# The prompt's attention scores of two heads, from zero-padded queries to two row tiles of 64 partitions

## The chip, the cores and the metric

The kernel runs on one core of one Trainium2 chip. A core has five engines that matter here: TensorE (PE in the profile, with its weight loads listed apart as PEld), VectorE (DVE), ScalarE (ACT), GpSimd (POOL) and SyncE (SP), which issues the DMAs. The metric is the device time of one execution in microseconds (us). Before the change it is 2594.43 us, the median of 3 runs from 2592.45 to 2596.81 us.

## The reference

The reference is one step of a two-layer decoder trunk, for a prompt of 1024 tokens and for 8 sequences of 8 sample tokens. Layer 0 is a Mamba-2 mixer, layer 1 is dilated sliding-window attention. The change touches only the attention of the prompt. Cut to that:

```python
DILATION_GROUPS = ((128, 1), (512, 4), (2048, 16))     # window, dilation
ATT_HEAD_DIM, ATT_HEADS, ATT_KV_HEADS = 64, 16, 4      # 4 query heads share a key head
def dilated_attend(q, kv_groups, rows_groups):
    for gi in range(N_DGROUPS):
        ...                                            # kg, vg: the keys and values of the window
        s = jnp.einsum('bqkrd,bqjkd->bqkrj', qg, kg)   # scores, contracted over 64
        s = jnp.where(valid[None, :, None, None, :], s, -jnp.inf)
        lse = jax.nn.logsumexp(s, axis=-1)
        pr = jnp.exp(s - lse[..., None])
        o = jnp.einsum('bqkrj,bqjkd->bqkrd', pr, vg)
        ...
    # the three groups are then merged by a softmax over their lse
```

## The kernel before

The attention of the prompt is stage 4. Its queries are taken in 24 units: 3 dilation groups of 8 units, each unit 128 query rows that have the same residue of the dilation. A unit sees either the keys of its own 128 rows alone (OWN, 13 units) or those of the 128 rows before it too (FULL, 11 units). `units4` runs them in this order: unit 0 OWN, 1 to 7 FULL, then 8 to 16 OWN and FULL in turn, then 17 to 23 OWN.

A unit has 8 steps, one for each pair of heads (a pair holds two query heads, `x` = 0 and 1, whose key heads lie in the lower and the upper 64 partitions of the same key tile). So stage 4 has 192 steps, 88 of FULL units and 104 of OWN units. For step A, each engine's program holds:

- PE (`section4_tensor`): the scores of step A (line 1837, one product per head, 256 columns in a FULL unit, 128 in an OWN unit; 4 instructions), then `turn_scores` for step A-2 (line 1801, transposes of the exponentials), then `values` for step A-3 (line 1818), and after steps 1, 3 and 5 of a unit one part of `turn` (lines 1788 and 1792), which transposes keys and queries of the next unit.
- DVE (`section4_vector`): mask and row maximum of step A for each head (line 1712), the negated maximum (line 1716), then `evacuate`, which copies the turned exponentials of step A-2 out of PSUM bank 6 (line 1696).
- ACT (`section4_scalar`): the exponentials of step A (line 1618); now and then `take`, which copies turned keys (line 1582) and queries (line 1586) from bank 7 into `kT` and `qT`, and `hand_out` (line 1595).

The scores go to banks 0 to 3, one bank for each head of two steps. The order on each engine is that of the code; the engines wait on semaphores. `turn_scores` of step A-1 waits until `evacuate` of step A-2 has freed bank 6; that in turn follows the mask of step A on DVE.

Before the change `qT` has, for each pair and each head, a full 128-partition block of which the other head's 64 partitions are zero. The product over 128 partitions then gives one head's scores. GpSimd writes these zeros once (line 1546), before anything else of stage 4, and ScalarE fills the 64 partitions of each head in a copy of its own (line 1586).

Of the kernel before, what the change touches and what calls it, by code (L numbers as in the profile page):

```python
# [25 lines left out]
P = 128  # L26
# [13 lines left out]
DI, HD, NH, NG, DS = 2048, 64, 32, 4, 128  # L40
# [12 lines left out]
AH, KVH, REP = 16, 4, 4  # L53
# [77 lines left out]
def trunk_kernel(nc, a, o, s):  # L131

    outer = ExitStack()
    with outer:
        def sem(name):
            return outer.enter_context(nc.semaphore(name))

        def sb_in(ctx):
            def sb(name, shape, dt=F32):
                return ctx.enter_context(nc.sbuf_tensor(name, shape, dt))  # L140
            return sb

        keep = sb_in(outer)
        bank = outer.enter_context(nc.psum_tensor("bank", [P, 8, 512], F32))
# [15 lines left out]
        h = keep("h", [P, NT, D])  # L160
# [78 lines left out]
        sb = sb_in(s1)  # L239
# [111 lines left out]
        def alone(eng):  # L351

            eng.sem_inc(q["waits_passed"], 1)
# [103 lines left out]
        def turn_of(i, times, const):  # L458

            return const if i is None else i * times + const  # L460
# [405 lines left out]
        def stage2_vector(dve, chain):  # L866
# [97 lines left out]
        sb = sb_in(s4)  # L964
        HP = AH // 2
# [2 lines left out]
        kn = sb("kn", [P, 2, KVH * HD])  # L968
        vv = sb("vv", [P, 2, 2, KVH * HD])
        kT = sb("kT", [P, 2, KVH // 2, 2, P])  # L970
        qT = sb("qT", [P, 2, HP, 2, P])
        win = sb("win", [P, 2 * P])
        pair = sb("pair", [P, P])
        sc = sb("sc", [P, 4, 512])
# [20 lines left out]
        f4 = {n: sem("att_" + n) for n in """m_landed s_full masked p_ready t_full pt_ready pv_done u_taken tr_full  # L995
            tr_ready kp_ready zeroed qz_landed os_stored qzs_ready
            ktr_full ktr_ready ss_full ss_masked se_ready rd_ready st_full spt_ready so_full so_ready schain""".split()}
# [84 lines left out]
        def third(pool, t):  # L1082

            pool.wait_ge(f5["w_ready"], t + 1)
            v = u6[t % 2][:, 2, :].rearrange("p (h d) -> p h d", h=AH)
            pool.tensor_tensor(v, v, bc(wts[:, t % 2, 4, 2, :], P, AH, HD), ALU.mult).then_inc(f5["third"], 1)
# [296 lines left out]
        def units4(eng, body):  # L1383

            body(None, 0, OWN, None, 0)
            body(None, 1, FULL, OWN, 1)
            with eng.Fori(0, 3) as i:
                body(i, 2, FULL, FULL, 1)
                body(i, 3, FULL, FULL, 2)
            body(None, 8, OWN, FULL, 0)  # L1390
            body(None, 9, FULL, OWN, 5)
            with eng.Fori(0, 3) as i:
                body(i, 10, OWN, FULL, 0)
                body(i, 11, FULL, OWN, 6)
            body(None, 16, OWN, FULL, 0)
            body(None, 17, OWN, OWN, 0)
            with eng.Fori(0, 2) as i:
                body(i, 18, OWN, OWN, 0)
                body(i, 19, OWN, OWN, 0)
            body(None, 22, OWN, OWN, 0)  # L1400
            body(None, 23, OWN, OWN, 0)

        def sequences(eng, body):

            with eng.Fori(0, NSEQ // 2 - 2) as i:
                for d in range(2):
                    body(i, d)
            for d in range(NSEQ - 4, NSEQ):
                body(None, d)
# [15 lines left out]
        def section4_sync(sp):  # L1425
# [13 lines left out]

            def load_queries(kv):  # L1440

                sp.wait_ge(f4["zeroed"], 3)
                for x in range(kv * REP, (kv + 1) * REP):
                    for g in range(NGR):
                        at = (x // (2 * REP) * 2 * REP + x % REP * 2 + kv % 2) * HD
                        src = s["q"][SEQ:TOK, g, at:at + HD].rearrange("(s t) d -> t s d", t=DSEQ)
                        sp.dma_start(qz[x * DSEQ:(x + 1) * DSEQ, :, g, kv // 2, (kv % 2) * HD:(kv % 2 + 1) * HD], src).then_inc(f4["qz_landed"], 16)
# [18 lines left out]
            def body(i, un, kind, before, nth):  # L1466
# [17 lines left out]
                if un in EARLY:  # L1484
                    load_queries(EARLY.index(un))
# [55 lines left out]

        def section4_gpsimd(pool):
            pool.wait_ge(j3["full"], UNITS3)
            for x in range(2):
                other = slice(64 * (1 - x), 64 * (1 - x) + 64)
                pool.memset(qT[other, :, :, x, :], 0.0).then_inc(f4["zeroed"], 1)
                pool.wait_ge(f4["zeroed"], x + 1)
            pool.memset(qz, 0.0).then_inc(f4["zeroed"], 1)

            def body(i, un, kind, before, nth):  # L1550
                if un < UN - 1:
                    nx = un + 1
                    pool.wait_ge(f4["tr_ready"], turn_of(i, 6, 3 * un + 1))
                    pool.wait_ge(f4["s_full"], turn_of(i, 32, 16 * un))
                    alone(pool)
                    pool.tensor_copy(kT[:, nx % 2, :, 0, :], kT[:, un % 2, :, 1, :]).then_inc(f4["kp_ready"], 1)

            units4(pool, body)
            pool.wait_ge(f4["qz_landed"], 16 * AH * NGR)
            pool.wait_ge(f4["t_full"], HP * UN)  # L1560

            def pick(i, d):

                if d > 1 or i is not None:
                    pool.wait_ge(f4["ktr_full"], turn_of(i, 14, 7 * max(0, d - 1)))
                alone(pool)
                pool.tensor_copy(qzs[:, d % 2, :, :, :], qz[:, bass.ds(turn_of(i, 2, d), 1), :, :, :].rearrange("p s g a d -> p (s g) a d")).then_inc(f4["qzs_ready"], 1)

            sequences(pool, pick)
            third(pool, 0)  # L1570
            third(pool, 1)

        def section4_scalar(act):

            def take(i, un, part):

                sl = un % 2
                act.wait_ge(f4["tr_full"], turn_of(i, 6, 3 * un + part + 1))
                if part == 0:
                    if un:  # L1580
                        act.wait_ge(f4["kp_ready"], turn_of(i, 2, un - 1))
                    act.copy(kT[:, sl, :, 1, :], bank[:, 7, 0:2 * P].rearrange("p (h n) -> p h n", h=2)).then_inc(f4["tr_ready"], 1)
                else:
                    for x in range(2):
                        hs_ = slice(64 * x, 64 * x + 64)
                        last = act.copy(qT[hs_, sl, 4 * (part - 1):4 * part, x, :], bank[hs_, 7, :].rearrange("p (h n) -> p h n", h=4))  # L1586
                    last.then_inc(f4["tr_ready"], 1)

            def hand_out(i, un, part):

# [4 lines left out]
                act.copy(ub[:, sl, part * 512:(part + 1) * 512], bank[:, 4 + part, :]).then_inc(f4["u_taken"], 1)  # L1595

            act.wait_ge(j3["rot_ready"], UNITS3)
            act.wait_ge(f4["zeroed"], 2)
            for part in range(3):
                take(None, 0, part)  # L1600

# [176 lines left out]
        def section4_tensor(pe):  # L1778
# [16 lines left out]
            def turn_scores(i, st0, kind):  # L1795
                pe.wait_ge(f4["p_ready"], turn_of(i, 16, st0 + 1))
                if st0 > 0:
                    pe.wait_ge(f4["pt_ready"], turn_of(i, 16, st0))
                for x in range(2):
                    for k in range(kind):  # L1800
                        last = pe.transpose(bank[:, 6, (x * kind + k) * P:(x * kind + k + 1) * P],  # L1801
                                            sc[:, st0 % 4, 256 * x + k * P:256 * x + (k + 1) * P], ident)
                last.then_inc(f4["t_full"], 1)
# [23 lines left out]
            def body(i, un, kind, before, nth):  # L1827
                sl, n = un % 2, kind * P
                pe.wait_ge(f4["tr_ready"], turn_of(i, 6, 3 * (un + 1)))
                if un:  # L1830
                    pe.wait_ge(f4["kp_ready"], turn_of(i, 2, un))
                for j in range(HP):
                    st0 = HP * un + j
                    if st0 > 1:
                        pe.wait_ge(f4["masked"], turn_of(i, 16, st0 - 1))
                    for x in range(2):
                        pe.matmul(bank[:, 2 * (st0 % 2) + x, 0:n], qT[:, sl, j, x, :],  # L1837
                                  kT[:, sl, j // REP, 2 - kind:2, :].rearrange("p a n -> p (a n)"), start=True, stop=True).then_inc(f4["s_full"], 1)
                    if st0 > 1:
                        turn_scores(i, st0 - 2, kind if j > 1 else before)  # L1840
                    if st0 > 2:
                        if j > 2:
                            values(i, un, j - 3, kind, nth)
                        else:
                            values(i, un - 1, j + HP - 3, before, 0)
                    if j in (1, 3, 5) and un < UN - 1:
                        turn(i, un + 1, j // 2)
# [217 lines left out]
        def _(pool):  # L2065
# [10 lines left out]
            with pool.Fori(0, NG) as g:  # L2076
# [36 lines left out]
                root(g * NT + LC, ROWS[LC])  # L2113
            stage2_gpsimd(pool)
            section4_gpsimd(pool)
            stage6_gpsimd(pool)

# [658 lines left out]
```

## Time and profile before

| what | value |
|---|---|
| median of 3 runs | 2594.43 us (2592.45 to 2596.81) |
| profiled execution, its own time | 2597.51 us |
| its span, first to last instruction | 2595.7 us |
| mean granted clock of TensorE | 0.969 of full speed |
| busy shares of the span | PE 94%, PEld 78%, DVE 55%, ACT 42%, POOL 17% |
| stage 4, first scores to the end of its last values | 1824.5 to 2195 us |

The page's busy shares are means over stages that differ; a matmul's end in the trace is modelled, and matmuls overlap one another, so PE counted as busy is not PE at its peak. How long a row of matmuls really holds PE is seen from the chain of work that ended last: there a group's time runs to the start of the next group, not to its own modelled end.

### The profile page before, as it was taken

Reading aid. Unit: us, or ns where it says so; the run is one execution under the profiler, and the core shown is the slowest. Engines: PE = TensorE matmul, PEld = TensorE weight load, DVE = VectorE, ACT = ScalarE, POOL = GpSimd, SP = SyncE. Lnnn points to the kernel's source line nnn. Section 1 sums busy time; section 2 is a strip of 40 time slices with the busy share of each in tenths; the row PEclk is TensorE's granted clock in tenths of the full one; section 3 lists DMA queues with packets and bytes.
Section 4 is the critical chain, followed back from the end, with each engine's and each line's share of the span. In section 5 each row is a group of like instructions: output and inputs, shape, how many; then the busy total and the mean of one; then the engine's idle time right before and its main releaser. Section 6 shows DMA issues by size and latency. Waiting matters only on the chain.

```text
span 2595.7 us, 38609 instructions
## 1 busy us (share of the span) xinstructions
PE 2429.4 (94%) x12776; PEld 2013.0 (78%) x12776; DVE 1427.7 (55%) x3033; ACT 1082.8 (42%) x2453; POOL 435.5 (17%) x327
## 2 busy tenths in 40 slices
PE   4699999999999779999999999999999988989998
PEld 3697797797798468887788888887898887667776
DVE  3267567667567413333463777751566665267632
ACT  3146346346346412332332333331667777353211
POOL 0006106106106100000120333310000000001100
PEclk8799999999999689999999999999999999889999
DMA  3032232232222653420142422321333347855210
GB/s 114 11 110 71 75 112 70 81 107 72 82 89 75 203 152 82 114 101 33 41 148 82 167 79 79 109 83 53 89 90 83 90 101 176 247 157 198 105 56 21
DMA packets 233453, 259.96 MB, mean 100 GB/s; under 512 B 33639, under 2 KB 176127, under 8 KB 233304
## 3 DMA queue, kind: packets, MB, share of 16 engines
q1 hardware_dynamic: 233304, 258.01, 32.8%
q8 instruction: 89, 1.46, 0.2%
q14 instruction: 60, 0.49, 0.1%
HBM read 192.46 MB, written 69.29 MB: 101 GB/s over the span
## 4 chain that ended last, share of the span: by engine, by line
PE 82%; DVE 7%; DMA 4%; issue 3%; ACT 2%; SPq 2%; POOL 0%; DVEq 0%; ACTq 0%; POOLq 0%
PE bank L781 7%; PE bank L780 7%; PE bank L782 7%; PE bank L1837 3%; PE bank L1818 3%; PE bank L2538 3%; PE bank L2539 3%; PE bank L2540 3%; PE bank L607 2%; PE bank L608 2%; PE bank L609 2%; PE bank L2592 2%; PE bank L1801 2%; PE bank L2705 2%; PE bank L2594 2%
## 5 line engine op out<-in xcount | busy, mean ns | idle before, releaser
L780 PE MATMUL bank<-wh,uH 128*128 128x512 f32 x792 | 308.5, 389 | 0.0
L782 PE MATMUL bank<-wh,uL 128*128 128x512 f32 x792 | 308.1, 389 | 0.0
L781 PE MATMUL bank<-wl,uH 128*128 128x512 f32 x792 | 308.1, 389 | 0.0
L1618 ACT ACTIVATE sc<-sc,nmx 128x128 f32<-128x128 f32 (+1 forms) x384 | 169.7, 443 | 98.5 <-DVE nmx L1716 97.2
L2538 PE MATMUL bank<-uH,wxh 128*128 128x364 f32 (+1 forms) x504 | 167.1, 331 | 10.1 <-DVE wxl L2351 10.1
L782 PEld LDWEIGHTS bank<-wh,uL 128*128 128x128 f32 x792 | 148.6, 188 | 30.9
L780 PEld LDWEIGHTS bank<-wh,uH 128*128 128x128 f32 x792 | 148.7, 188 | 30.8
L781 PEld LDWEIGHTS bank<-wl,uH 128*128 128x128 f32 x792 | 148.7, 188 | 30.7
L2539 PE MATMUL bank<-uL,wxh 128*128 128x364 f32 (+1 forms) x504 | 166.4, 330 | 0.0
L2540 PE MATMUL bank<-uH,wxl 128*128 128x364 f32 (+1 forms) x504 | 166.2, 330 | 0.0
L1837 PE MATMUL bank<-kT,qT 128*128 128x128 f32 (+1 forms) x768 | 162.1, 334 | 1.4 <-ACT qT L1586 1.4
L2094 POOL TENSOR_TENSOR mix<-mix,cbm 128x1024 f32<-128x1024 f32 (+1 forms) x36 | 95.6, 2657 | 374.0 <-DVE cbm L2405 372.0
L703 POOL TENSOR_TENSOR hs<-hs,mhalf 128x8 f32<-128x8 f32 (+1 forms) x54 | 108.5, 2009 | 236.4 <-DVE hs L936 236.4
L1818 PE MATMUL bank<-vv,pT 128*128 128x64 f32 x1120 | 146.8, 266 | 0.1
L1818 PEld LDWEIGHTS bank<-vv,pT 128*128 128x128 f32 x1120 | 140.1, 192 | 0.6 <-DVE pT L1696 0.3
L1712 DVE CUSTOM_DVE_ANT_0 sc<-bank,win 128x256 f32<-128x256 f32 (+1 forms) x256 | 87.9, 381 | 89.8 <-PE bank L1837 77.5
L607 PE MATMUL bank<-woh,yh 128*128 128x512 f32 x288 | 115.8, 402 | 16.4 <-DVE yl L581 13.9
L2592 PE MATMUL bank<-wzh,uH 128*128 128x512 f32 x288 | 125.1, 434 | 3.5 <-ACT zs L2238 3.5
L1837 PEld LDWEIGHTS bank<-kT,qT 128*128 128x128 f32 x768 | 116.4, 194 | 6.4 <-issue 1.7
L854 ACT ACTIVATE raws<-bank,rstd 128x512 f32<-128x512 f32 (+1 forms) x54 | 37.1, 688 | 197.3 <-PE bank L782 178.9
L608 PE MATMUL bank<-wol,yh 128*128 128x512 f32 x288 | 114.3, 397 | 0.0
L609 PE MATMUL bank<-woh,yl 128*128 128x512 f32 x288 | 113.9, 396 | 0.0
(341 smaller groups left out, 5624.5 us busy)
## 6 DMA issues: line engine op xcount, KB each, us to landing
mix<-scratch_acum SPq DMA_DIRECT2D x32, 512.0 KB, 3.8
yin<-scratch_yT SPq DMA_DIRECT2D x16, 1024.0 KB, 5.9
wr<-in_a_in_w SPq DMA_DIRECT2D x16, 1024.0 KB, 7.5
wx<-in_m_in_w SPq DMA_DIRECT2D x24, 512.0 KB, 3.9
scratch_q<-rot SPq DMA_DIRECT2D x48, 256.0 KB, 2.0
qn<-scratch_q SPq DMA_DIRECT2D x48, 256.0 KB, 3.5
scratch_u<-ub SPq DMA_DIRECT2D x48, 256.0 KB, 2.9
u<-scratch_u SPq DMA_DIRECT2D x24, 512.0 KB, 5.4
```

The costliest lines, as they stand in the source:

```text
L607: pe.matmul(to, high[:, k, :], woh[j][:, k, :], start=(k == 0), stop=False)
L608: pe.matmul(to, high[:, k, :], wol[j][:, k, :], start=False, stop=False)
L780: pe.matmul(bank[:, t % 3, :], high, whigh, start=(k == 0), stop=False)
L781: pe.matmul(bank[:, t % 3, :], high, wlow, start=False, stop=False)
L782: last = pe.matmul(bank[:, t % 3, :], low, whigh, start=False, stop=(k == KT - 1))
L1618: last = act.activation(v, v, ACT.Exp, bias=nmx[:, sl, head(j, x):head(j, x) + 1], accum_out=mxs[:, sl, AH + head(j, x):AH + head(j, x) + 1])
L1818: last = pe.matmul(bank[:, 4 + hd // 8, (hd % 8) * HD:(hd % 8 + 1) * HD], pT4[:, st0 % 2, (x * kind + k) * P:(x * kind + k + 1) * P], vv[: ...
L1837: pe.matmul(bank[:, 2 * (st0 % 2) + x, 0:n], qT[:, sl, j, x, :], kT[:, sl, j // REP, 2 - kind:2, :].rearrange("p a n -> p (a n)"), start=T ...
L2538: pe.matmul(to, wxh[:, f % 2, k, :], uH[:, k, c0:c1], start=(k == 0), stop=False)
L2539: pe.matmul(to, wxh[:, f % 2, k, :], uL1[:, k, c0:c1], start=False, stop=False)
L2540: last = pe.matmul(to, wxl[:, f % 2, k, :], uH[:, k, c0:c1], start=False, stop=(k == KT - 1))
L2592: pe.matmul(bank[:, 4, :], uH[:, k, ts], wzh[:, k, :], start=(k == 0), stop=False)
```

## The change

`qT` holds both heads of a pair in one block: head 0 in partitions 0 to 63, head 1 in 64 to 127, without zeros. The scores of a head are then one product over 64 partitions, `rows` 0 to 63 or 64 to 127 of both operands, so that the two products of a pair use two row tiles of the array. The two zeroing memsets and the waits for them go, and `take` copies a part of the queries in one copy over 128 partitions in place of two over 64. A block `below_win` fills the memory that `qT` gives up, so that all other tiles stay where they were.

```diff
-        qT = sb("qT", [P, 2, HP, 2, P])
+        qT = sb("qT", [P, 2, HP, P])
+        sb("below_win", [P, 2 * HP * P])
...
-                sp.wait_ge(f4["zeroed"], 3)
+                sp.wait_ge(f4["zeroed"], 1)
...
-            for x in range(2):
-                other = slice(64 * (1 - x), 64 * (1 - x) + 64)
-                pool.memset(qT[other, :, :, x, :], 0.0).then_inc(f4["zeroed"], 1)
-                pool.wait_ge(f4["zeroed"], x + 1)
             pool.memset(qz, 0.0).then_inc(f4["zeroed"], 1)
...
-                    for x in range(2):
-                        hs_ = slice(64 * x, 64 * x + 64)
-                        last = act.copy(qT[hs_, sl, 4 * (part - 1):4 * part, x, :], bank[hs_, 7, :].rearrange("p (h n) -> p h n", h=4))
-                    last.then_inc(f4["tr_ready"], 1)
+                    act.copy(qT[:, sl, 4 * (part - 1):4 * part, :], bank[:, 7, :].rearrange("p (h n) -> p h n", h=4)).then_inc(f4["tr_ready"], 1)
...
-            act.wait_ge(f4["zeroed"], 2)
...
                     for x in range(2):
-                        pe.matmul(bank[:, 2 * (st0 % 2) + x, 0:n], qT[:, sl, j, x, :],
-                                  kT[:, sl, j // REP, 2 - kind:2, :].rearrange("p a n -> p (a n)"), start=True, stop=True).then_inc(f4["s_full"], 1)
+                        rows = slice(HD * x, HD * (x + 1))
+                        pe.matmul(bank[:, 2 * (st0 % 2) + x, 0:n], qT[rows, sl, j, :],
+                                  kT[rows, sl, j // REP, 2 - kind:2, :].rearrange("p a n -> p (a n)"), start=True, stop=True).then_inc(f4["s_full"], 1)
```

On ScalarE, from the queries of unit 0 to those of unit 1 (COPY into `qT` are the queries, ACTIVATE the exponentials), before:

```order
L1582 COPY kT<-bank 128x2x128
L1586 COPY qT<-bank 64x4x128 x4
L1618 ACT_TABLE_LOAD
L1618 ACTIVATE sc,mxs<-sc,nmx 128x128 x4
L1582 COPY kT<-bank 128x2x128
L1618 ACTIVATE sc,mxs<-sc,nmx 128x128 x4
L1586 COPY qT<-bank 64x4x128 x2
```

The same place after the change:

```order
L1579 COPY kT<-bank 128x2x128
L1581 COPY qT<-bank 128x512 x2
L1611 ACT_TABLE_LOAD
L1611 ACTIVATE sc,mxs<-sc,nmx 128x128 x4
L1579 COPY kT<-bank 128x2x128
L1611 ACTIVATE sc,mxs<-sc,nmx 128x128 x4
L1581 COPY qT<-bank 128x512
```

Each pair of copies into `qT` has become one; nothing else moved. On TensorE, in unit 1, the scores, the transposes and the values stand in the same order after the change as before. After it:

```order
L1831 MATMUL bank<-kT,qT 128x256 x2
L1794 MATMUL bank<-cst,sc 128x128 x2
L1811 MATMUL bank<-vv,pT 128x64 x2
L1781 MATMUL bank<-cst,kn 128x128 x2
L1831 MATMUL bank<-kT,qT 128x256 x2
L1794 MATMUL bank<-cst,sc 128x128 x4
```

The sizes that the rows give are those of the output; what changed is that each of the two products of a step now has 64 rows of weights, and that everything between two such pairs still has 128.

## Rows read from the trace of the kernel before

**Rows 1.** The page: span, engines' busy time, and granted clock in 40 slices.

```profile
span 2595.7 us, 38609 instructions
PE 2429.4 (94%) x12776; PEld 2013.0 (78%) x12776; DVE 1427.7 (55%) x3033; ACT 1082.8 (42%) x2453; POOL 435.5 (17%) x327
...
PEclk8799999999999689999999999999999999889999
```

**Rows 2.** Busy time in four stretches of stage 4.

```profile
core 0: us, PE busy (x) PEld busy (x) DVE busy (x) ACT busy (x) POOL busy (x), PEclk, DMA share, GB/s
1824.50:1836.16 11.66, 10.78 (x74) 10.26 (x75) 7.21 (x46) 10.01 (x35) 0.40 (x1) 0.82 0.26 64
1836.16:1966.34 130.18, 129.77 (x952) 116.93 (x952) 90.11 (x336) 86.00 (x274) 2.80 (x7) 1.00 0.34 81
1966.34:2107.07 140.73, 131.75 (x1020) 120.25 (x1020) 95.61 (x434) 101.08 (x351) 3.60 (x9) 1.00 0.38 90
2107.07:2195.00 87.93, 76.05 (x634) 70.63 (x633) 60.53 (x339) 71.42 (x273) 2.00 (x5) 1.00 0.56 133
```

**Rows 3.** Waits in stage 4 (1824.5 to 2195 us): total, times, longest.

```profile
PEld bank L1801 <- issue: 36.9, 88, 0.8
PE bank L1801 <- DVE pT L1696: 18.3, 55, 0.6
```

**Rows 4.** The chain in FULL unit 2 (start, us, what).

```profile
1863.55 0.87 PE bank L1837 x4
1864.41 0.44 PE bank L1801 x4
1864.85 0.84 PE bank L1818 x8
1865.69 0.92 PE bank L1837 x4
```

**Rows 5.** The chain in OWN unit 19.

```profile
2142.32 0.45 PE bank L1837 x4
...
2143.71 0.44 DVE pT L1696
2144.14 0.14 issue
2144.28 0.41 PE bank L1801 x2
```

**Rows 6.** The chain in the Mamba stage, around products over 64 partitions.

```profile
669.93 1.09 PE bank L2683 x8
671.01 0.59 PE bank L2667 x4
671.60 0.44 PE bank L2608 x4
```

**Rows 7.** Timeline of weight loads, transposes of 128 and 24 rows in turn.

```profile
2198.28 0.14 PEld L1873 LDWEIGHTS bank<-cst,ck 128*128 128x128 f32 x1 [0.42 <-ACT uT L1640]
2198.54 0.13 PEld L1874 LDWEIGHTS bank<-cst,nk 24*128 24x128 f32 x1
2198.70 0.14 PEld L1873 LDWEIGHTS bank<-cst,ck 128*128 128x128 f32 x1
```

**Rows 8.** Timeline of weight loads of products with 8 columns (line 2630).

```profile
178.24 0.96 PEld L2630 LDWEIGHTS bank<-cst,u 64*128 64x128 f32 x8 [0.23 <-issue]
```

**Rows 9.** Groups by line and shape, stage 4.

```profile
L1586 ACT COPY qT<-bank 64x512 f32<-64x512 f32 x92 | 53.0, 576 | 1.2
L1595 ACT COPY ub<-bank 128x512 f32<-128x512 f32 x47 | 26.9, 573 | 0.6
```

**Rows 10.** The chain at the start of stage 4.

```profile
1814.56 3.86 DMA kn<-scratch_kv
...
1820.84 0.58 ACT qT L1586
```

**Rows 11.** Timeline, GpSimd's zeros in `qT`.

```profile
1812.74 3.82 POOL L1546 MEMSET qT<- 64x2048 f32 x2 [92.25 <-PE bank L782]
```

## The prediction

> **What bounds the kernel now.** I read the page first, then the chain of waits around line 1837, then stage 4 cut into stretches. The page says that PE is busy 94% of the span and that the clock stands at its upper level through stage 4 [rows 1]. That is a mean; what a shorter or longer score product is worth depends on the stretch [rows 2]. In units 1 to 7 (FULL, 56 steps) PE is busy 129.77 of 130.18 us: every 0.1 us that PE gains or loses in a step arrives at the end. In units 8 to 16 (32 FULL and 40 OWN steps) it idles 9.0 of 140.7 us, in units 17 to 23 (56 OWN steps) 11.9 of 87.9 us. These waits are of one kind: the transposes of line 1801 wait 55 times for DVE's copy of line 1696, and their weight loads stand idle 36.9 us in 88 places [rows 3]. The chain shows the pattern as pairs of steps [rows 5]: scores of step A (0.45 us), then DVE's mask and copy until 2144.14, then `turn_scores` of A-1 at 2144.28, values, a part of `turn`, and the scores of A+2. The scores of A+1 lie inside the 1.5 us between 2142.77 and 2144.28, in which PE has only those scores, two transposes and four values to do; they are off the path.
>
> **What a step costs now.** In a FULL unit four score instructions hold PE for 0.87 to 0.92 us, so 0.22 each, in an OWN unit 0.45, so 0.11 each; eight values hold it 0.84, four transposes 0.44 [rows 4, 5].
>
> **What the change adds: two changes of the array's shape in each step.** The scores now have 64 rows of weights, the transposes and values around them 128. The Mamba stage already does this, in a place where four transposes take the 0.44 us that they take in stage 4. There eight products over 64 partitions with 128 columns hold PE 1.09 us, where eight score instructions of the same columns take 2 x 0.45 = 0.90: going in costs 0.19. The four transposes behind them take 0.59 where the next four take 0.44 [rows 6]: coming out costs 0.15 [rows 6]. That is 0.34 for a round trip. The other bound is a pair of transposes of 128 and 24 rows, whose loads are 0.42 us apart [rows 7]; at 0.11 each they should be 0.22 apart, so two changes cost 0.20 there. I take 0.30 for a round trip, near the first, which has the very form of the new product. What I see in both is that a load does not start under the last product of the other shape, as it does otherwise; the price is that uncovered time.
>
> **What it may take away: two tiles at work at once.** No row here shows two row tiles side by side, so this is bounded. A step's four instructions stand in the order head 0 first pass, head 0 second pass, head 1 first pass, head 1 second pass. If products start in order and one tile does one at a time, only head 0's second and head 1's first pass can overlap: a step of four becomes one of three, a gain of one instruction, 0.22 (FULL) or 0.11 (OWN). The bounds are 0 and two instructions, 0.44 and 0.22. In OWN steps a load is as long as a product: eight products of only 8 columns still need loads over 0.96 us, about 0.11 each [rows 8]. If the loads of the two tiles follow one another, the OWN step gains nothing. I take one instruction for FULL and none for OWN.
>
> The Trainium skill says in TensorE: Matmul & The Clock Gate, section "The mechanism", that products start and end in program order and that a weight load may be drawn ahead where row groups differ; that is the overlap of one instruction. In its section "Measured speedup vs the span model" packed tiles take as long as one product plus about 4 ns for each tile; by that rule the gain would be two instructions, and no run here shows it yet.
>
> **ScalarE, GpSimd, SyncE.** The 92 copies of 64x512 that the stretch holds (0.576 us each, 53.0 us) become 46 of 128x512; ACT's own copy of that size takes 0.573 [rows 9]. ACT loses about 26 us of work, but no wait of PE in stage 4 ends on it [rows 3], so this is worth nothing after the start. At the start two such pairs lie on the chain, of copies of 0.58 [rows 10]: 2 x 0.6 = 1.2 us gained. The memsets ended at 1816.56, before the first keys landed at 1818.42 [rows 10, 11], and the code issues the sample part's queries, the other waiter for them, only from unit 8 on; both are worth nothing.
>
> **The sum, against the profiled execution (2597.5 us).**
> - Units 1 to 7: 56 x (0.30 - 0.22) = +4.5.
> - Units 8 to 16: I count half of the steps as saturated: 16 FULL x 0.08 = +1.3, 20 OWN x 0.30 = +6.0. The others go in pairs, where only the change into the scores of A lies on the path, while the idle 0.4 to 0.8 us in front of line 1801 takes up the rest: 10 OWN pairs x 0.19 = +1.9, 8 FULL pairs x (0.19 - 0.22) = -0.2. Together +9.0.
> - Units 17 to 23: 28 pairs x 0.19 = +5.3.
> - Unit 0: 4 x 0.30 + 2 x 0.19 = +1.6. The start: -1.2.
>
> Sum: +19.2, so 2616.7. That execution is 3.1 us above the median of the runs; on the median it is 2613.6, so 2614 us. With the round trip between 0.20 and 0.34 this case runs from about 2600 to 2618: 96 saturated steps and 48 pairs move with it.
>
> **Rivals.**
> 1. The tiles do not overlap at all, and the change does not do what it says. Without the 0.22 in 72 saturated FULL steps and 8 pairs the sum is +36.8: 2631 us. For it: between a load and its product and the next load all rows here go one after another. Against it: the two tiles share no partition and no PSUM bank.
> 2. The loads overlap too, so that OWN steps also gain one instruction: 24 saturated steps and 40 pairs x 0.11 = 7.0 less, +12.2: 2607 us; with the round trip at 0.20 this is about no change.
> 3. Faster: each tile runs its two instructions beside the other's. Beyond my case 80 x 0.22 + 64 x 0.22 = 31.7 less, -12.5: 2582 us. It decides as soon as head 1's first pass starts with head 0's first, and then the 0.44 of a FULL step beats the round trip. Against it speaks the order of the four; nothing in the trace shows it.
> 4. Going from one tile to the other waits too. No overlap, and 0.15 more in 96 steps and 48 pairs: 36.8 + 21.6 = +58: 2653 us. The Trainium skill speaks against it: in TensorEngine Tiling (Array Packing), section "Key Properties", only a change of the mode drains, not one of the tile.
>
> **Chances.** My case 0.38, no overlap 0.24, loads overlap 0.18 (0.08 of it within 0.2% with the cheap round trip), full overlap 0.13, a wait between the tiles 0.07. 0.2% is 5.2 us, what a measurement here can tell from no change. A remainder of 0.01 goes to faster: 0.14 faster, 0.08 same, 0.78 slower. The range from 2596 to 2635 takes in my case, no overlap and overlapping loads with both ends of the round trip, some 0.8 together; it leaves out rivals 3 and 4.
>
> **What the profile after would show.** Right: the weight loads of the scores and of the transposes behind them each start some 0.2 us after the product before them, in every step; a FULL step without `turn` takes about 2.2 us where it took 2.14 (1863.55 to 1865.69) [rows 4]; head 1's first product starts together with head 0's second; in units 17 to 23 the idle time in front of the transposes shrinks and the pair grows by 0.2; the copies of queries take 0.57 each, 48 of them. Wrong: loads that go on under the products of the other shape, or all four score products of a FULL step done within 0.45 us (rival 3), or each started only when the one before has ended (rivals 1 and 4).

## The result: 0.2% slower, by the clock

| | before | changed |
|---|---|---|
| median of 20 runs | 2594.84 us (2589.40 to 2600.51) | 2601.97 us (2592.20 to 2639.80) |
| ratio, 95% interval | | 1.0022 [1.0012, 1.0031] |
| profiled execution, its span | 2597.51, 2595.7 us | 2602.58, 2600.8 us |
| mean granted clock | 0.969 | 0.964 |
| stage 4, first scores to last values | 1824.53 to 2195.79 (371.25) | 1820.10 to 2203.20 (383.10) |

Here and below the ratio counts only executions within 1.5% of the fastest of their kernel, and the medians count all; where the two differ, the executions left out are those with the lowest mean clock.

The change costs 5.1 us of span: stage 4 begins 4.4 us earlier, lasts 11.85 us longer, and what follows it takes 2.3 us less. The page after, to be laid beside [rows 1]; in its second row PEld has fallen from 2013.0 to 1975.0 us:

```profile
span 2600.8 us, 38559 instructions
PE 2429.0 (93%) x12776; PEld 1975.0 (76%) x12776; DVE 1431.4 (55%) x3033; ACT 1051.2 (40%) x2405; POOL 431.8 (17%) x325
...
PEclk8799999999999789999999999999899989989999
```

The same four stretches as in [rows 2], changed kernel (the columns are those of rows 2):

```profile
1820.10:1837.87 17.77, 15.42 (x75) 12.07 (x75) 7.52 (x46) 9.50 (x34) 0.40 (x1) 0.50 0.32 79
1837.87:1964.90 127.03, 126.00 (x952) 99.40 (x951) 90.08 (x337) 75.76 (x260) 2.80 (x7) 0.97 0.36 83
1964.90:2114.88 149.98, 139.69 (x1019) 112.10 (x1018) 95.31 (x433) 89.87 (x333) 3.60 (x9) 0.91 0.36 85
2114.88:2203.20 88.32, 77.45 (x639) 63.06 (x639) 60.97 (x339) 62.69 (x261) 2.68 (x6) 1.00 0.57 134
```

Units 1 to 7 took 130.18 us and take 127.03; units 17 to 23 took 88.7 to their last values and take 88.3. The loss sits in unit 0 (11.63 to 17.76 us) and in units 8 to 16 (140.7 to 150.0), just where the clock column has fallen most: from 0.82 to 0.50 and from 1.00 to 0.91. In units 1 to 7 it has fallen to 0.97, in units 17 to 23 it is 1.00 in both kernels. Cut finer, before has one stretch at 1.2 GHz around stage 4, from 1815.1 for 13.7 us; after has three, from 1811.9 for 34.1, from 1982.6 for 10.2 and from 2081.6 for 17.1 us.

**At the upper clock the step is shorter.** The chain in FULL unit 3, to be laid beside [rows 4]:

```profile
1881.06 0.84 PE bank L1811 x8
1881.90 0.63 PE bank L1831 x4
1882.54 0.02 issue
1882.56 0.63 PE bank L1794 x4
1883.19 0.84 PE bank L1811 x8
1884.03 0.44 PE bank L1785 x4
1884.47 0.63 PE bank L1831 x4
1885.10 0.59 PE bank L1794 x4
```

Scores 0.87 to 0.92 have become 0.63, transposes 0.44 have become 0.58 to 0.63. The step without `turn` lasts 2.06 (1875.45 to 1877.51) where it lasted 2.14, the one with `turn` 2.57 (1881.90 to 1884.47) where it lasted 2.68, and each of the units 2 to 7 is 0.83 to 0.94 us shorter. The weight loads and products of one step, from the timeline (start, length of the group, what):

```profile
1859.44 0.30 PEld L1831 LDWEIGHTS bank<-kT,qT 64*128 64x128 f32 x4
1859.45 0.70 PE L1831 MATMUL bank<-kT,qT 64*128 64x256 f32 x4
```

Four loads lie within 0.30 us; [rows 8] has 0.96 for eight. The single records inside these groups start, in us after 1859.000: products 0.446 and 0.453 (the first pass of either head), then 0.766 and 0.773 (the second passes, which carry the signals of the finished products); loads 0.445, 0.451, 0.553, 0.560. So both heads run side by side in both passes, 7 ns apart. That is rival 3.

In OWN units the two effects cancel. The chain in OWN unit 19, beside [rows 5]; the first line is a further one of the chain before, the start of DVE's mask after the scores at 2142.32:

```profile
2143.00 0.22 DVE sc L1712
...
2146.79 0.47 PE bank L1831 x4
2147.47 0.23 DVE sc L1705
2147.78 0.20 DVE sc L1705
2148.20 0.44 DVE pT L1689
2148.63 0.14 issue
2148.77 0.41 PE bank L1794 x2
2149.18 0.39 PE bank L1811 x4
```

The scores hold PE 0.47 us (0.45 before), and DVE's mask starts 0.68 us after the scores, as before. A pair of steps, from scores to scores, lasted 2.21 + 1.06 us and lasts 2.09 + 1.18.

**At the lower clock it is not.** The stretches of the third row above in which the clock fell, and the one ahead of the first fall:

```profile
1978.10:1982.60 4.50, 3.35 (x25) 2.27 (x24) 2.89 (x13) 3.14 (x13) 0.00 (x0) 1.00 0.51 140
1982.60:1992.80 10.20, 10.20 (x44) 7.80 (x44) 4.28 (x18) 3.80 (x12) 0.00 (x0) 0.50 0.38 87
...
2081.60:2098.60 17.00, 17.00 (x74) 13.47 (x73) 7.14 (x27) 6.01 (x19) 0.00 (x0) 0.50 0.39 92
```

In these PE is busy for 10.20 of 10.20 and 17.00 of 17.00 us: nothing waits, everything is slow. Before the first fall PE had waited for keys; in the kernel before it waits in the same place of unit 9 too (3.50 of 4.40 us busy), and its clock stays at 1.00 there and after it:

```profile
1979.50:1983.90 4.40, 3.50 (x23) 2.79 (x22) 2.85 (x13) 2.96 (x12) 0.00 (x0) 1.00 0.57 149
1983.90:1992.00 8.10, 7.89 (x56) 6.97 (x57) 4.66 (x18) 5.40 (x19) 0.00 (x0) 1.00 0.32 75
```

Unit by unit (after minus before, us): 0 +6.14, 1 +2.03, units 2 to 7 -5.18 together, 9 +3.49, 11 -0.71, 13 -0.60, 15 +6.88, all other units together -0.20. Units 11 and 13 are the same work as 9 and 15 without a fall in them, so the two falls cost about 3.5 + 0.7 and 6.9 + 0.7, 11.8 us.

### The profile page after: what moved, and what is told of

Read it like the earlier page. It is cut to its first block, busy times and chain, and to the rows that moved or that the text cites. A ratio compares the mean times of both kernels' runs of the same rounds, so it can differ in the third digit from the quotient of the medians.

```text
span 2600.8 us, 38559 instructions
## 1 busy us (share of the span) xinstructions
PE 2429.0 (93%) x12776; PEld 1975.0 (76%) x12776; DVE 1431.4 (55%) x3033; ACT 1051.2 (40%) x2405; POOL 431.8 (17%) x325
## 4 chain that ended last, share of the span: by engine, by line
PE 82%; DVE 7%; DMA 3%; issue 3%; ACT 2%; SPq 2%; DVEq 0%; POOL 0%; ACTq 0%; POOLq 0%
PE bank L782 7%; PE bank L780 7%; PE bank L781 7%; PE bank L1811 3%; PE bank L2532 3%; PE bank L1831 3%; PE bank L2533 3%; PE bank L2534 3%; PE bank L1794 3%; PE bank L607 2%; PE bank L609 2%; PE bank L608 2%; PE bank L2586 2%; PE bank L2588 2%; PE bank L2587 2%
## 5 line engine op out<-in xcount | busy, mean ns | idle before, releaser
L1811 PE MATMUL bank<-vv,pT 128*128 128x64 f32 x1120 | 154.0, 275 | 0.1
L1811 PEld LDWEIGHTS bank<-vv,pT 128*128 128x128 f32 x1120 | 148.6, 201 | 0.4 <-DVE pT L1689 0.3
L1794 PE MATMUL bank<-cst,sc 128*128 128x128 f32 x560 | 106.8, 301 | 17.9 <-DVE pT L1689 17.0
L1831 PE MATMUL bank<-kT,qT 64*128 64x128 f32 (+1 forms) x768 | 120.3, 392 | 0.8 <-ACT qT L1581 0.8
```

Of the source, the lines that this page charges most:

```text
L1811: last = pe.matmul(bank[:, 4 + hd // 8, (hd % 8) * HD:(hd % 8 + 1) * HD], pT4[:, st0 % 2, (x * kind + k) * P:(x * kind + k + 1) * P], vv[: ...
L1831: pe.matmul(bank[:, 2 * (st0 % 2) + x, 0:n], qT[rows, sl, j, :], kT[rows, sl, j // REP, 2 - kind:2, :].rearrange("p a n -> p (a n)"), star ...
```

## The experiments

That the products gain at the upper clock is common to all theories that the expectations name; they differ in where the loss comes from. Theory A lays the loss at the start of stage 4 to a memset of GpSimd that holds up the keys. Rival B, and Theory C after it, lay the loss to the granted clock, which products over 64 partitions bring down. Rival D has the changes of shape or the pauses of PE do this.

e1 to e4 ran on one chip, e5 to e8 on a second, e9 to e11 on a third and e12 on a fourth, each beside the kernel before. The changed kernel itself ran beside e5 to e7 alone (as e8), so the times of e1 and e2 are compared with the kernel before alone.

**e1: the 64-partition products alone**, in the memory layout of before, with all zeros and copies kept.

```diff
-  pe.matmul(..., qT[:, sl, j, x, :], kT[:, sl, ...
+  rows = slice(HD * x, HD * (x + 1))
+  pe.matmul(..., qT[rows, sl, j, x, :], kT[rows, sl, ...
```

> The kernel before with its zero-padded queries, its two memsets and its two copies kept; only the two score products of a step take 64 partitions each. Theory A (two losses): at full clock a FULL step is 0.08 to 0.10 us shorter and an OWN pair the same, and the loss at the start of stage 4 (units 0 and 1 take 37.3 us after the change, 29.1 before) comes from GpSimd's zeros of qz, which now lie under VectorE's last copy (4.81 us instead of 1.39), hold up the DMA queue and make TensorE wait 2.3 us for unit 1's keys. Then units 0 and 1 take 28 to 30 us here, units 2 to 7 0.85 us less each, and the kernel is at about 2588 us if the clock holds in units 9 to 16, up to 2600 if it falls there. Rival B (the clock goes down because of the products over 64 partitions alone): units 0 and 1 take about 37 us here too, and the kernel is at about 2602 us.

Measured: 2630.85 us (2595.92 to 2639.54), ratio 1.0109 [1.0062, 1.0156]. The FULL units 2 to 7 gain 0.84 to 0.94 each, as in the change. Around stage 4 the clock is low from 1812.3 for 34.1 us, and three times later, longest from 2143.4 for 44.4 us, where units 19 to 21 lose 5.91, 6.43 and 3.69. Its executions had mean clocks of 0.945 to 0.967, those of the kernel before beside it 0.967 to 0.974. So the products alone are enough for both, the gain and the loss, without the copies and zeros. That the time is 29 us above the 2602 of Rival B is not explained: the changed kernel did not run on this chip. The longest of the low stretches:

```profile
2143.00:2188.00 45.00, 44.87 (x216) 36.79 (x216) 20.38 (x112) 25.27 (x90) 0.80 (x2) 0.51 0.42 98
```

**e2: the changed kernel, its remaining memset later.** Without the two zeroing memsets, GpSimd's memset for the sample part starts earlier, at 1809.88, beside DVE's last copy of stage 3. These are the copy in the changed kernel, and what waits for keys in unit 0:

```profile
1810.57 4.81 DVE L945 COPY rot<-raws 64x512 f32<-64x512 f32 x1 [5.00 <-ACT raws L850]
...
1823.60 0.69 PE L1781 MATMUL bank<-cst,kn 128*128 128x128 f32 x2 [2.27 <-DMA kn<-scratch_kv]
```

Before, that copy took 1.39 us. e2 puts one wait ahead of the memset:

```diff
+            pool.wait_ge(j3["rot_ready"], UNITS3)
             pool.memset(qz, 0.0).then_inc(f4["zeroed"], 1)
```

> The changed kernel, with GpSimd's memset of qz put behind VectorE's last copy of stage 3. Theory A: the last copy takes 0.4 to 1.4 us instead of 4.81, units 0 and 1 take about 29 us instead of 37.3, and the kernel is 6 to 9 us faster than the changed one: 2593 to 2596 us. Rival B: the copy is short too, but the clock stays low as long as before, units 0 and 1 take 35 us or more, and the kernel stays at about 2600 us.

Measured: 2632.59 us (2600.74 to 2657.60), ratio 1.0116 [1.0078, 1.0155].

```profile
1809.81 0.42 DVE L945 COPY rot<-raws 64x512 f32<-64x512 f32 x1 [5.00 <-ACT raws L850]
...
1821.20 0.69 PE L1782 MATMUL bank<-cst,kn 128*128 128x128 f32 x2 [0.37 <-DMA kn<-scratch_kv]
```

The copy takes 0.42, the wait for keys 0.37 in place of 2.27, and unit 0 takes 15.87 in place of 17.76. The mechanism is real and worth 1.9 us in unit 0, but it is not the main reason why the kernel is slower: the low stretch at the start still lasts 30.7 us, and units 0 and 1 take 35.9 us, as Rival B has it and not the 29 of Theory A. What e2 is worth in time is not shown, since the changed kernel did not run on this chip. (The profiled execution is the top of the range, with a further low stretch of 180.9 us from 2076.9, so only its start is read.)

**e3: 64 partitions in FULL units only; e6: in OWN units only; e7: in units 1 to 7 only.** All are e1 with a condition on `rows`; e6 has `kind == OWN`.

```diff
+  rows = slice(HD * x, HD * (x + 1)) if kind == FULL else slice(0, P)              # e3
+  rows = slice(HD * x, HD * (x + 1)) if kind == FULL and un < PT else slice(0, P)  # e7, PT is 8
```

> The kernel before, with products over 64 partitions in FULL units alone; OWN units keep the products over 128. Theory A: 88 FULL steps gain 0.06 to 0.10 us each, 5 to 9 us, less what a fall of the clock in units 9 to 15 costs: 2586 to 2592 us. Rival B: units 0 and 1 as before, since unit 0 has no such product; units 9 to 15 lose their clock as after the change (4 to 11 us): 2593 to 2600 us.

> The kernel before, with products over 64 partitions in OWN units alone. Theory C: the FULL units gain nothing, the clock stays low longer at the start and falls in units 9 to 23 in some runs: 2600 to 2645 us. If the falls came from the FULL units, it would be at 2594 to 2598 us.

> The kernel before, with products over 64 partitions in units 1 to 7 alone (FULL units one after another, TensorE without idle time). Theory C: these seven units gain 0.85 us each, no other unit changes, and the clock's falls are those of the kernel before: 6 us less, 2588 to 2591 us. If FULL units lower the clock too: 2595 us or more.

| | median (range) | ratio [95%] | low stretches in stage 4 |
|---|---|---|---|
| e3 | 2590.56 (2585.76 to 2598.47) | 0.9981 [0.9970, 0.9992] | 13.7 at the start; 3.4; 3.4 |
| e6 | 2602.35 (2596.40 to 2631.05) | 1.0053 [1.0026, 1.0081] | 27.3 at the start |
| e7 | 2589.84 (2581.85 to 2593.71) | 0.9976 [0.9966, 0.9987] | 10.2 at the start |

The same edit is faster in one kind of unit and slower in the other. In e3 and e7 units 1 to 7 gain 0.84 to 0.95 each, 6.2 us together, and the time of e7 follows: 0.24% of 2594 is 6.2. In the traced execution of e6 no unit but 0 and 1 changes by more than 0.5 us (+3.7 and +1.2), and these two lie in the long low stretch. That execution took 2600.33 us at a mean clock of 0.969; three of e6's ten took 2619 to 2631 us at 0.954 to 0.960, lower than in any of the 12 executions of e3 (0.963 to 0.972) or of e7 (0.968 to 0.974). So e6 has more low stretches in other executions than the trace shows; where they lie is not known. Units 1 to 7 in e7, and unit 0 in e6:

```profile
1833.90:1957.90 124.00, 122.27 (x952) 96.82 (x951) 90.16 (x337) 86.35 (x275) 2.82 (x7) 1.00 0.36 85
```

```profile
1820.20:1838.00 17.80, 17.71 (x82) 14.04 (x83) 7.77 (x47) 11.23 (x39) 0.40 (x1) 0.50 0.16 41
```

**e4: no overlap.** The changed kernel with both heads' products in partitions 0 to 63, so that head 1's scores are computed from head 0's queries and keys; the shape is the same, the second tile is gone.

```diff
-  rows = slice(HD * x, HD * (x + 1))
+  rows = slice(0, HD)
```

> The changed kernel, with both score products of a step in partitions 0 to 63, so that they share one row tile; head 1's scores are then computed from head 0's queries and keys, so its output is not the reference's. The trace after the change shows the two heads' first passes 7 ns apart and their second passes 7 ns apart: a step's products take the time of two instructions instead of four. If that is the gain, each of 72 saturated FULL steps grows by 0.43 us, and OWN pairs by 0.2: +31 +10, so 2640 to 2650 us. If the two tiles are not what saves the time, it stays at about 2602 us.

Measured: 2944.41 us (2940.42 to 2945.43), ratio 1.1341 [1.1327, 1.1356], some 300 us more than expected. The expectation left the clock out: it falls at 1814.8 and stays down for 730 us. A third of that time, with PE busy throughout:

```profile
1876.20:2112.00 235.80, 235.80 (x829) 186.25 (x828) 78.55 (x288) 68.75 (x222) 2.41 (x6) 0.50 0.16 38
```

The chain gives the overlap's worth where both kernels run at 1.2 GHz in OWN steps. Without the second tile, in e4:

```profile
2453.19 1.15 PE bank L1831 x4
2454.34 0.62 PE bank L1794 x2
2454.96 0.74 PE bank L1811 x4
```

and with it, in a further run of the changed kernel (e8, below):

```profile
2144.84 0.73 PE bank L1831 x4
2145.57 0.62 PE bank L1794 x2
2146.19 0.75 PE bank L1811 x4
```

1.15 - 0.73 = 0.42, two instructions of 0.21. The overlap is complete in OWN steps too. And an idle PE is not needed for the clock to stay low: it does so here with PE busy throughout.

**e5 and e9: more work for PE in OWN units.** The changed kernel with two further products in every odd step of an OWN unit, over 128 partitions in e5 and over 64 in e9; their results go nowhere.

```diff
+  for x in range(2 if kind == OWN and j % 2 else 0):
+      pe.matmul(bank[...], kT[:, sl, 0, 1, :], kT[:, sl, 1, 1, :], ...)        # e5
+      pe.matmul(bank[...], kT[0:HD, sl, 0, 1, :], kT[0:HD, sl, 1, 1, :], ...)  # e9
```

> The changed kernel, and in every second step of the OWN units two more products over all 128 partitions (128 columns, into unused columns of the score banks, results not used), placed where TensorE waits for VectorE afterwards. Theory C (the granted clock falls because two row tiles feed the array for only half the time, and the rest of an OWN unit is too little): with the old amount of full-array work back, the clock holds in units 9 to 23, the rise at the start comes after some 14 us as before, units 0 and 1 take about 29 to 32 us, and the kernel is at 2588 to 2596 us. Rival D (the changes of the array's shape or the pauses make it fall): the falls stay, and the kernel is at 2600 to 2640 us.

> As the changed kernel with two more products in every second step of the OWN units, but these over 64 partitions (0 to 63) instead of 128: the same count of instructions and columns, half of the array. Theory C (what counts is how much of the array works, not how long TensorE is busy): the clock falls in units 9 to 23 and at the start as in the changed kernel, single runs from 2600 to 2650 us, mean granted clock 0.945 to 0.968. If busy time alone counts, it goes like the run with products over 128 partitions: 2595 to 2610 us, mean clock 0.965 to 0.974, no run above 2615 us.

e5: 2600.65 us (2594.65 to 2609.62), 1.0029 [1.0016, 1.0043]; e9: 2604.49 (2598.19 to 2609.44), 1.0047 [1.0034, 1.0060]. In both the falls of units 9 to 23 are gone: unit 9 takes 17.49 and 17.41 where the changed kernel took 21.94, unit 15 takes 17.33 and 17.24 for 25.23. No execution of either took more than 2610 us, where 5 of the 32 of the changed kernel took 2631 to 2640. The OWN units pay for it with up to 1.4 us each (unit 23 with 2.3). Stage 4 from 1984 on, in e9:

```profile
1984.00:2205.00 221.00, 209.95 (x1725) 173.68 (x1725) 147.82 (x728) 144.66 (x557) 5.70 (x15) 1.00 0.45 107
```

So from unit 9 on it is not the amount of 64-partition work that decides, since e9 has more of it than the change, against what its expectation gave Theory C; more work for PE in the OWN units goes with a clock that stays up, in either shape. Nor are the changes of shape enough for these falls (Rival D): the added products stand beside others of their shape, so there are as many changes as in the change. At the start the two differ: the low stretch lasts 17.1 us in e5 and 44.4 in e9, each in one execution.

**e8: the changed kernel once more.** No edit.

> The changed kernel once more, beside the others of this call. Theory C: its time depends on how often the clock falls in units 9 to 23: single runs between 2590 and 2660 us, the low ones as fast as the kernel before or faster, and the mean granted clock falls as the time rises.

2601.57 us (2588.60 to 2635.08), 1.0011 [0.9999, 1.0023], an interval that no longer excludes no change. Its single runs lie along the clock: 2589 us at a mean clock of 0.972, 2594 at 0.969, 2607 at 0.963, 2635 at 0.947. The instructions are the same in each; the 46 us between the first and the last go with the clock. In the profiled run the low stretches are 30.7 us at the start, then 10.2, 3.4 and 23.9, and not where they were: unit 15 has none now, units 19 and 20 have one.

```profile
2139.00:2163.00 24.00, 24.00 (x117) 19.72 (x117) 11.41 (x63) 12.32 (x47) 0.40 (x1) 0.50 0.31 73
```

**e10 and e11: the round trip by itself.** The kernel before with one small product of 8 columns ahead of each step's scores, over 64 partitions (e10) or 128 (e11).

```diff
+  pe.matmul(bank[..., 256:264], kT[0:64, sl, 0, 1, :], kT[0:64, sl, 1, 1, 0:8], ...)    # e10; e11 has 0:128
   for x in range(2):
       pe.matmul(..., qT[:, sl, j, x, :], ...
```

> The kernel before (scores over 128 partitions), and ahead of each step's scores one more product over 64 partitions with 8 columns (2 instructions, result not used): two changes of the array's shape in each step and nothing else. Round trip 0.34 us plus two loads of 0.11 us: FULL steps of units 2 to 7 grow by 0.50 to 0.60 us, so a unit takes 22.8 to 23.6 us instead of 18.7 to 18.9; the kernel is 40 to 60 us slower than before, 2635 to 2655 us. The clock holds, if changes of shape do not lower it.

> The control to the run before it in this call: the same small product over 128 partitions, so no change of shape. Two loads of 0.11 us: a unit of 2 to 7 takes 20.2 to 20.7 us, and the kernel is 12 to 25 us slower than before. The difference between the two, per FULL step, is the price of a round trip: 0.30 to 0.34 us expected.

e10: 2666.09 us (2654.06 to 2668.20), 1.0271 [1.0252, 1.0291]; e11: 2620.64 (2618.55 to 2622.07), 1.0109 [1.0094, 1.0123]. In units 2 to 7 the clock is 1.00 in both; a unit takes 22.34 us in e10 and 20.31 in e11, so a round trip costs 2.03/8 = 0.25. The chain of e10, then that of e11:

```profile
1916.35 0.32 PE bank L1836 x2
1916.66 1.06 PE bank L1838 x4
1917.72 0.44 PE bank L1801 x4
```

```profile
1918.35 0.18 PE bank L1836 x2
1918.53 0.97 PE bank L1838 x4
1919.49 0.44 PE bank L1801 x4
```

The low stretch at the start lasts 41.0 us in e10 and 13.7 in e11, and units 0 and 1 together 47.8 and 32.4. Neither has an overlap of tiles, and their counts of products are the same; so one small product over 64 partitions in each step is enough to keep the clock down there. Whether its 64 rows of weights do it or the two changes of shape that it brings to each step, this pair does not tell; e5 against e9, with as many changes in both, speaks for the rows.

**e12: units 1 to 7 as in e7, and a warm start.** 31 products of the identity with itself, over 128 partitions, into the free bank 6 around the three parts of `turn` ahead of unit 0, where PE waits for keys. A wait that stood behind them moves ahead of them.

```diff
+  pe.wait_ge(j3["raw_ready"], UNITS3)
   for part in range(3):
+      for _ in range((20, 3, 4)[part]):
+          pe.matmul(bank[:, 6, 0:P], ident, ident, start=True, stop=True)
       turn(None, 0, part)
-  pe.wait_ge(j3["raw_ready"], UNITS3)
+  for _ in range(4):
+      pe.matmul(bank[:, 6, 0:P], ident, ident, start=True, stop=True)
```

> The version with products over 64 partitions in units 1 to 7 alone, and 31 small products over 128 partitions (identity by identity, 128 columns, result not used) at the start of stage 4, where TensorE waits for the first keys (20) and for ScalarE's copies (11). Theory C: the clock does not fall at the start (10 to 14 us low without them), the transposes of unit 0 and its first steps run at full clock, 2 to 4 us less than without: 2585 to 2588 us. If the fall at the start does not come from TensorE's wait: no change, 2589 to 2591 us, or up to 2 us more for products that end after the keys have landed.

2585.71 us (2584.37 to 2590.71), 0.9966 [0.9954, 0.9978]; mean clock 0.972 to 0.976. In the traced execution no part of stage 4 is at 1.2 GHz, and unit 0 takes 11.05 us (11.63 before). The wait for keys and unit 0, e12:

```profile
1814.00:1825.20 11.20, 8.82 (x73) 8.18 (x72) 1.39 (x1) 3.38 (x6) 9.33 (x4) 1.00 0.81 209
1825.20:1836.30 11.10, 9.14 (x76) 8.35 (x76) 7.29 (x46) 10.07 (x35) 0.40 (x1) 1.00 0.33 89
```

It beats the kernel before, and the change did not. The products in the wait were not tried without the 64-partition units, so how the gain beyond e7's (0.9976) divides is not shown.

## Why the prediction was right in its sign and wrong in its working

| us | forecast | measured | at the upper clock |
|---|---|---|---|
| start (scores of unit 0) | -1.2 | -4.4, of it -1.2 from the copies | |
| unit 0 | +1.6 | +6.1 | not seen |
| units 1 to 7 | +4.5 | -3.2 | -6.2 (e7) |
| units 8 to 16 | +9.0 | +9.3 | about -2.8 (four FULL units at -0.7) |
| units 17 to 23 | +5.3 | -0.4 | -0.4 |
| span | +19.2 | +5.1 | |

Of the remaining 3.2 us of the start 2.9 come from ahead of stage 4, where the last product lies earlier by a shorter low stretch around 900 us (6.8 us in place of 20.5), and 0.4 from keys that land sooner after it; the 2.3 us behind stage 4 are likewise the clock's. None of this work is touched by the edit.

**The step that failed: "I take one instruction for FULL and none for OWN."** It was two and two (0.44 and 0.22 us). The bounds held it, and rival 3 described it, to its condition: head 1's first pass starts with head 0's first. I put rival 3 at 0.13 because the order of the four instructions spoke against it. The records of e4, where all four share a tile, stand in that order (every second one carries the signal). The order does not bind across tiles: head 1's first pass, third in it, starts 7 ns behind the first and 313 ns ahead of the second. The Trainium skill's rule in TensorE: Matmul & The Clock Gate, section "Measured speedup vs the span model" (one product and some 4 ns for each further tile), comes near these 7 ns; its section "The mechanism", with which my sum agreed, says that products start in program order; the records of this two-pass product differ from that, and the measurement decides.

**The term that was missing: the clock.** I read 1.00 in [rows 2], passed over the 0.82 of unit 0, and carried it over. None of my cases held that the clock itself would answer to the change. It costs here, by unit: 11.8 us in units 9 and 15, and in units 0 and 1 about 8.2 - 1.9 (the memset) + 0.9 (what unit 1 gains elsewhere) = 7.2; 19 us in all, an estimate from these rows. Without it and the memset's 1.9 stage 4 would be 11.85 - 20.9 = -9 us, near rival 3's -12.5, of which -1.2 is the start. By this estimate the kernel is slower only because of it, and e7, whose units 1 to 7 keep the clock, shows the gain alone. That the span grew at all, as forecast, is therefore luck: the gain that I took for a price was turned into a loss by a term that I did not have. That units 8 to 16 came out at +9.3 against +9.0 is chance, two falls of the clock in place of 20 slow OWN steps.

**The round trip: right in kind, and nearly in size.** Going in costs 0.63 - 0.44 = 0.19, coming out 0.59 - 0.44 = 0.15, as in [rows 6]; with a lone small product 0.25 (e11 against e10). I took 0.30. The Trainium skill's rule in TensorEngine Tiling (Array Packing), section "Key Properties", that a change of the mode drains and one of the tile does not, agrees with both: no wait between the tiles (rival 4) and 0.34 around them.

**OWN pairs: the wrong reason.** The step into the scores of A was to lie on the path with 0.19. It does, but the scores themselves lose 0.22 by the overlap, so that DVE's mask starts after 0.68 us as before, and the pair (3.27 us) does not grow. The waits in front of the transposes stayed too, against "the idle time shrinks" ([rows 3]: 18.3 us, 55 times):

```profile
PEld bank L1794 <- issue: 47.9, 106, 1.0
...
PE bank L1794 <- DVE pT L1689: 17.0, 51, 0.6
```

**The start and the zeros.** The copies are right: 0.567 us each, and 1.2 us gained, as predicted. From the first transposes of stage 4 to the first scores 6.07 us (1818.46 to 1824.53) have become 4.88 (1815.22 to 1820.10).

```profile
1818.46 0.69 PE L1788 MATMUL bank<-cst,kn 128*128 128x128 f32 x2 [5.78 <-DMA kn<-scratch_kv]
...
1815.22 0.69 PE L1781 MATMUL bank<-cst,kn 128*128 128x128 f32 x2 [5.41 <-DMA kn<-scratch_kv]
...
L1581 ACT COPY qT<-bank 128x512 f32<-128x512 f32 x47 | 26.7, 567 | 5.7 <-PE bank L1785 5.6
```

"The memsets are worth nothing" was wrong: I looked at who waits for the removed zeros, and not at what the memset behind them would then lie beside. It cost 1.9 us (e2).

**The rivals.** No overlap and a wait between tiles fell by the four records and by e4 against e8; overlapping loads hold, as a part of rival 3.

**What stays open.** It is shown that products over 64 partitions in OWN units bring the clock down (e6 against e7, e1 against the kernel before; at the start e10 against e11), that it can stay down without PE idling (e4), and that with more work in OWN units it stayed up from unit 9 on, in either shape (e5, e9). In units 1 to 7, FULL units one after another, they do not: in e7 it is 1.00 throughout. What the chip counts for it is not settled, nor where a fall comes: of one kernel, the traced executions of the change and of e8 had falls in different units, and each kernel here has one trace. The rows of weights and the changes of shape were not parted by a pair of their own.

## What to carry to other kernels

Two row tiles of 64 partitions do run two passes each side by side, and the change of shape around them costs 0.25 to 0.34 us each time at 2.4 GHz: pack where the products saved are longer than that, and keep the others in one shape. Price a change of a product's shape at the clock that the stage will then have, not at the one it has: compare the granted clock of both kernels stretch by stretch before explaining any difference by instructions. And when an instruction is removed, ask what the next one on its queue will now run beside.

## What the runs showed of the hardware

- The four records of two 64-partition products of a FULL step start 0, 7, 320 and 327 ns after the first: the passes alternate between the tiles.
- PE can stand at 1.2 GHz while busy without a break: 235.80 of 235.80 us in e4, 24.00 of 24.00 in e8.
- The low stretch around the start of stage 4 lasted 10.2 to 13.7 us in the four kernels with no 64-partition products in unit 0 (before, e3, e7, e11), 27.3 to 44.4 in seven with them (the change, e1, e2, e6, e8, e9, e10); e5, which adds work over 128 partitions there, had 17.1. In e4 it went on for 730 us, and in e12, with products in the wait, there was none.
- A copy of 64x512 on DVE took 0.42 us with no GpSimd memset beside it, 1.39 in the kernel before, where the zeroing memsets run, and 4.81 in the changed one. In the changed kernel the memset ran from 1809.88 to 1815.10 and the copy from 1810.57 to 1815.38: it ended 0.28 us after the memset. In the kernel before it likewise ended (1814.82) 0.28 us after the first zeroing memset (1814.54). The Trainium skill says in SBUF — State Buffer, section "SBUF: two separate sides", that GpSimd and some kinds of VectorE instruction share a port pair which the first to start holds for its whole instruction; both traces agree.
